# Spreads and a rotation on TensorE: one product of 128 columns, or two of 64

## The reference

```
h = h + concat([ya, yb]) @ w_out;  h = h + rmsnorm(p @ w_pe) * sigmoid(h @ w_pg)
k = partial_rope(k, pos)      # the first 16 of 64 channels of a head are rotated
y = swa_attention(q, k, v, sinks) * silu(gate);  x = x + y @ w_out
return rmsnorm(x, final_g)
```

## Time and profile before

| | |
|---|---|
| runs, us | 1776.14, 1776.02, 1781.95 |
| profiled execution, span, us | 1780.4 |
| TensorE busy (matmul) | 1759.6 us, 99% |
| VectorE busy | 1312.3 us, 74% |
| ScalarE busy | 899.0 us, 50% |
| GpSimd busy | 39.9 us, 2% |
| mean granted clock of TensorE | 0.999 of full |
| DMA | 326.07 MB, 183 GB/s |

### The profile page before, as it was taken

One profiled execution on the slowest core, in us unless ns is written; L12 is line 12 of the kernel. 1 busy time (PEld: TensorE's weight loads), 2 busy tenths in 40 slices (PEclk: granted clock), 3 DMA queues, 4 the chain that ended last, 5 costly groups with the idle time before them and its releaser, 6 DMA issues.

```text
span 1780.4 us, 35691 instructions
## 1 busy us (share of the span) xinstructions
PE 1759.6 (99%) x14349; PEld 1678.8 (94%) x14349; DVE 1312.3 (74%) x2087; ACT 899.0 (50%) x1326; POOL 39.9 (2%) x48
## 2 busy tenths in 40 slices
PE   8999999999999999999999999999999999999997
PEld 8999999999999999999999899898989999999876
DVE  7899899976779987998677765556565657566754
ACT  5433665545544355556465454545455443655653
POOL 0000000000000000000000110000100000000000
PEclk9999999999999999999999999999999999999999
DMA  7666545555656665456556656665655566455553
GB/s 232 187 206 193 190 143 174 192 188 185 192 177 209 192 199 151 146 186 206 189 191 197 201 179 203 187 189 170 206 162 170 190 190 193 142 158 169 172 189 130
DMA packets 200082, 326.07 MB, mean 183 GB/s; under 512 B 14911, under 2 KB 66319, under 8 KB 199821
## 3 DMA queue, kind: packets, MB, share of 16 engines
q1 hardware_dynamic: 197085, 320.85, 58.0%
q10 hardware_dynamic: 2864, 3.36, 0.6%
HBM read 320.42 MB, written 2.69 MB: 181 GB/s over the span
## 4 chain that ended last, share of the span: by engine, by line
PE 86%; DVE 9%; ACT 1%; issue 1%; DMA 1%; ACTq 0%; DVEq 0%; SPq 0%
PE g L495 67%; PE g L506 11%; DVE w_lo L902 4%; DVE cacc L1148 3%; PE att L620 2%; PE att L641 2%; PE att L596 2%; DMA turned<-q 1%; ACT w_hi L1531 1%; ACTq L1519 0%; PE att L793 0%; DVE u L996 0%; DMA stage<-in_w_in_dram 0%; ACT L1540 0%; DVE q L923 0%
## 5 line engine op out<-in xcount | busy, mean ns | idle before, releaser
L902 DVE TENSOR_TENSOR w_lo<-stage,w_hi 128x1024 fp32r<-128x1024 f32 x577 | 707.6, 1234 | 388.8 <-ACT w_hi L1531 388.1
L1531 ACT CAST w_hi<-stage 128x1024 fp32r<-128x1024 f32 x577 | 598.2, 1050 | 595.3 <-PE g L495 373.7
L495 PE MATMUL g<-a_hi,w_hi 128*128 128x256 f32 x2496 | 703.9, 282 | 2.4 <-DVE w_lo L902 1.5
L495 PE MATMUL g<-a_hi,w_lo 128*128 128x256 f32 x2496 | 695.0, 278 | 0.0
L495 PE MATMUL g<-a_lo,w_hi 128*128 128x256 f32 x2496 | 694.9, 278 | 0.0
L495 PEld LDWEIGHTS g<-a_hi,w_hi 128*128 128x128 f32 x2496 | 472.1, 189 | 11.8 <-issue 9.5
L495 PEld LDWEIGHTS g<-a_lo,w_hi 128*128 128x128 f32 x2496 | 470.6, 189 | 0.0
L495 PEld LDWEIGHTS g<-a_hi,w_lo 128*128 128x128 f32 x2496 | 469.7, 188 | 0.5 <-issue 0.2
L495 PE MATMUL g<-b_hi,w_hi 128*128 128x256 f32 x1440 | 403.6, 280 | 0.4 <-DVE w_lo L902 0.3
L495 PE MATMUL g<-b_hi,w_lo 128*128 128x256 f32 x1440 | 400.4, 278 | 0.0
L495 PE MATMUL g<-b_lo,w_hi 128*128 128x256 f32 x1440 | 400.4, 278 | 0.0
(11 more groups left out here) (230 smaller groups left out, 1368.1 us busy)
## 6 DMA issues: line engine op xcount, KB each, us to landing
stage<-in_fox_w_in_dram SPq DMA_DIRECT2D x128, 512.0 KB, 3.8
stage<-in_w_in_dram SPq DMA_DIRECT2D x112, 512.0 KB, 3.8
stage<-in_swa_w_in_dram SPq DMA_DIRECT2D x72, 512.0 KB, 3.9
stage<-in_w_in_dram SPq DMA_DIRECT2D x128, 256.0 KB, 3.1
stage<-in_w_out_dram SPq DMA_DIRECT2D x64, 512.0 KB, 4.2
stage<-in_w_pg_dram SPq DMA_DIRECT2D x64, 512.0 KB, 3.9
stage<-in_fox_w_out_dram SPq DMA_DIRECT2D x32, 512.0 KB, 4.5
stage<-in_swa_w_out_dram SPq DMA_DIRECT2D x32, 512.0 KB, 4.0
```

The costliest lines, as they stand in the source:

```text
L495: mm = pe.matmul(acc[:, j * S:(j + 1) * S], w[:, slot, c0 + j * P:c0 + (j + 1) * P], xx[:, k, :], start=st and m == 0 and j % 2 == 0, stop ...
L902: dve.tensor_tensor(w_lo[:, slot, :], stage[:, slot, :], w_hi[:, slot, :].bitcast(F32), ALU.subtract).then_inc(*t.inc("w_split"))
L1531: act.copy(w_hi[:, slot, :], stage[:, slot, :]).then_inc(*t.inc("w_rounded"))
```

## The change

A helper `by_halves` issues a product twice: with columns 0 to 63 of the stationary tile into partitions 0 to 63, then with columns 64 to 127 into partitions 64 to 127. Both read the same moving tile. It takes the place of the full product in `spread_rs`, `ln_sum(0)`, `ln_spread` and `turn_keys`. The semaphore is raised by the second half. The four one-column products of `stats` and of L733 stay.

```diff
--- before.py
+++ after.py
@@ -547,6 +547,13 @@
             XY = ((a_hi, a_lo), (b_hi, b_lo))
             misc_reader = ["vec_done"]
 
+            def by_halves(dst, cols, w, moving, first=True):
+
+                for at in (0, HD):
+                    mm = pe.matmul(dst[at:at + HD, cols], w[:, at:at + HD], moving, start=first, stop=True,
+                                   skip_group_check=True)
+                return mm
+
             def taken():
 
                 pe.wait_ge(*t.again("gemm_free", 1))
@@ -569,8 +576,7 @@
                     pe.wait_ge(*t.see("rs_ready"))
                     pe.wait_ge(*t.again(misc_reader[0]))
                     for i, root in enumerate(roots):
-                        mm = pe.matmul(MB[:, i * S:(i + 1) * S], ones[:, :], root[:, :, :].rearrange("p b s -> p (b s)"),
-                                       start=i == 0, stop=True, skip_group_check=True)
+                        mm = by_halves(MB, slice(i * S, (i + 1) * S), ones, root[:, :, :].rearrange("p b s -> p (b s)"), i == 0)
                     mm.then_inc(*t.inc("rs_spread"))
                     t.skip("rs_taken")
                     misc_reader[0] = "rs_taken"
@@ -725,7 +731,7 @@
                             pe.wait_ge(*t.again(misc_reader[0]))
                             misc_reader[0] = "ln_centred"
                             t.skip("ln_centred", 2)
-                            mm = pe.matmul(MB[:, 0:S], ones[:, :], mean[:, :], start=True, stop=True)
+                            mm = by_halves(MB, slice(0, S), ones, mean[:, :])
                         else:
                             pe.wait_ge(*t.again("s_free"))
                             pe.wait_ge(*t.again("t_free"))
@@ -738,8 +744,8 @@
                 def ln_spread():
 
                     pe.wait_ge(*t.see("ln_pow"))
-                    pe.matmul(SB[:, 0:S], ones[:, :], diag2[:, :, :].rearrange("p b s -> p (b s)"), start=True,
-                                    stop=True).then_inc(*t.inc("ln_spread"))
+                    mm = by_halves(SB, slice(0, S), ones, diag2[:, :, :].rearrange("p b s -> p (b s)"))
+                    mm.then_inc(*t.inc("ln_spread"))
                     t.skip("ln_scaled", 2)
 
                 keys = lambda j: kk[half(j):half(j) + HD, 0 if (j // 4) % 2 == j % 2 else 1, :]
@@ -838,7 +844,7 @@
                 taken()
                 pe.wait_ge(*t.again(misc_reader[0]))
                 misc_reader[0] = "rope_used"
-                pe.matmul(MB[:, :], rot, kk[:, 0, :], start=True, stop=True).then_inc(*t.inc("roped"))
+                by_halves(MB, slice(0, 2 * S), rot, kk[:, 0, :]).then_inc(*t.inc("roped"))
                 t.skip("rope_used")
 
             def swa_there():
```

## The result

Five runs of the changed kernel lie between 1785.15 and 1787.54 us, median 1786.69; five of the kernel before between 1776.02 and 1781.95, median 1778.32. The ratio is 1.004 with a 95% interval of 1.0022 to 1.0057: 8 us slower, where 2.9 were forecast, and above the forecast range of 1775.5 to 1785.0. The profiled execution of the changed kernel took 1787.02, with a span of 1785.2.

A forecast was written before the change was run, and what follows sets the result against it. The prediction took TensorE's queue, mostly the L495 product line (67% of the span), as the bound. Costs at eleven places summed to +2.87 us, ratio 1.0016, giving 1779.0 us from the median 1776.14, range 1775.5 to 1785.0.

The forecast's parts named there:

- The price of a place: At each changed product: two column halves in place of one full product add 0.35 us, 1.01 instead of 0.66.
- the waiting one: Spread at 382 us that waits for GpSimd's diag: edge partly paid already, 0.87 becomes 1.01, 0.15 us added.
- the rotation: The changed product with 512 columns: 1.09 us becomes 1.44, 0.35 added.
- the two spreads in a row: Two L572 products at one place, 975.20 to 976.29: 1.09 us becomes 1.44, 0.35 added.
- The third rival (halves one after another): At all changed products: halves do not overlap, +10.2 us, 1786.3; chance 0.06.
- the first (free edges): At all changed places: the edges cost nothing, time 1776.1 to 1776.3; chance 0.08.
- the four together last about 0.86: Sign in the changed profile: a spread's four instructions start in pairs and last 0.27 + 0.215 + 0.38 us.
- The readers: VectorE behind L741's spread: L1239 starts 0.15 us later in both layers, costed at nothing; wait about 0.8 instead of 0.67.
- The waits in front of L733: Behind the two L728: TensorE's idle 0.17 and 0.21 us swallow part of the 0.35, net 0.18 and 0.14.
- The sum: All eleven places: six at 0.35, three at 0.15, L728 0.18 + 0.14, together +2.87 us.
- Shifts that I see no mechanism for: No place named: a remaining case for changes in time without a known cause; chance 0.04.
- The two times of before: Base of the forecast: profiled span 1780.4, 4.3 us above the runs' median 1776.14; ratio 1.0016 applied to the median.

## Why the prediction was wrong, point by point

- **The price of a place** was right: 1.01 instead of 0.66 at the first spread, 1.03 instead of 0.87 at the waiting one; the rotation went from 1.09 to 1.45 (1483.26 to 1484.71), 1.44 was forecast, the two spreads in a row only to 1.36 (979.65 to 981.01) instead of 1.44. The halves run in pairs although they read the same moving tile, and edges stand on both sides. The third rival (halves one after another) and the first (free edges) are out. The sign "the four together last about 0.86" was a slip of one step too many: one product in halves is two steps, 0.27 + 0.38 = 0.65, which is what the block shows; the price of 1.01 had counted them rightly.
- **The readers** were right: VectorE waits 0.83 at L741's spread, 0.8 was forecast.
- **The waits in front of L733** (L739 of after) did not shrink:

```profile
330.24 0.28 PE L495 MATMUL g<-b_lo,w_hi 128*128 128x256 f32 x1
330.55 0.60 PE L739 MATMUL att<-ones,mean 128*128 128x1 f32 x4
```

It starts 0.31 after the last L495, against 0.29. The 83 products between L728 and L733 ran at 113.3 instead of 117.8 ns (73 instead of 71 in the window of 8 us), since the halves, unlike the full product, left the fast pace as it was; TensorE made up there, 83 x 4.4 ns = 0.37 us, what it had lost. So the place cost next to nothing instead of 0.18, by a path that was not forecast.

- **The step that failed is "The sum"**: it adds what the eleven places cost and lets L495 run on as before, with a plain step of 0.12. The rows had both steps side by side, 0.12 in the earlier trace rows and 0.11 in the earlier trace rows, and I read them as rounding. A difference of 4.4 ns is nothing at a place, but a stretch of 1018 products (850.7 to 966.0) makes 4.5 us of it, more than all edges together. "Shifts that I see no mechanism for" got a chance of 0.04; the two paces were there to be read.
- **The two times of before**: I scaled from the profile (1780.4) to the median (1776.14) without asking for the 4.3 us between them. The profiled execution had one of the two stretches slow, and its time, 1782.1 with the 1.7 us around the span, lies in the middle group of runs; the median of three was a run of the lowest. That the gap is that stretch follows from the groups, not from a profile of such a run.
- The account with the missing term, from before's lower group of some 1778: two slow stretches, 1061 x 4.4 ns and 991 x 4.4 ns, +9.0; the places, 7 x 0.35 + 0.27 + 3 x 0.16 = +3.2; the stretches behind L741 fast, 2 x -1.4, and behind L728 -0.37 each. Together +8.7 against the 8.4 measured. The forecast had only the second term, less 0.4 for waits that it thought would shrink. It is a sum of sizes, not a proof term by term: shorter stretches in the attention and behind the second layer's first spread (0.4 to 1.7 us each) also change pace from kernel to kernel, and some of them from profile to profile.

What is shown: the two paces, that each of the two long stretches is worth 4.5 to 4.7 us by its pace, that a kernel without the halves takes the changed kernel's time when both are slow and one with more halves takes the time of before when both are fast, and that the changed kernel has both slow in both of its profiles. What stays open: what in TensorE makes the two paces, why four steps of halves exchange them, and why two steps left the pace as it was where they met the fast one (21 of 21 places in the profiles) while from the slow one they went either way (18 slow, 13 fast; slow all six times at 382 and 850, fast behind L741 at 337 in the changed kernel).

## What to carry to other kernels

Before pricing an edit in a dense stream by the cost at its place, count the products in a window behind the place, in more than one profile: the stream may have two paces, and an interruption picks one. Where the runs of a kernel lie in groups with even distances, find out which stretch differs before taking their median for a base. A restart that leads to the fast pace can be worth more than the interruption costs. Read the pace in front of the interruption too: here a full product that did not wait always left the slow pace and a group of four steps of halves always exchanged the two. For two steps of halves and for a full product that waits no rule was found; they have to be measured place by place.

## What the runs showed that was not expected

- L495 (128x128 stationary, 256 moving columns) runs at 113.3 or 117.8 ns at the full clock and keeps the pace from one interruption to the next, for over 120 us in the longest stretch.
- A full f32 product that did not wait left the slow pace (30 of 30 places); one that waited for GpSimd left either (1022 or 1061, 991 or 953 products, in two profiles of one program). A group of four steps of halves exchanged the pace (118 of 118).
- Issuing two spreads 1.4 us later, which took a wait of 0.2 us away at each, brought the kernel to 1787.0, into the highest of its three groups, 8.8 us over the median of the lowest.
- A pair of column halves costs 0.35 us for its two edges among full-width products, here as in the attention.
